# Seven stationary operands of a two-block transformer step placed at other byte remainders

## The reference

```python
def memory_cross_attention(h, mem_h, w_xq, w_xkv, w_xo):
    kv = mem_h @ w_xkv            # mem_h: 256 memory rows of 2048; w_xkv 2048 x 4096
    ...
def conv_glu_ffn(h, w_gate, w_up, conv_w, conv_b, w_down):   # first block, D_FF = 5632
    gate = causal_dwconv(h @ w_gate, conv_w, conv_b)
    return (jax.nn.silu(gate) * (h @ w_up)) @ w_down
def second_block(...):            # its feed-forward, D_FF_2 = 8192
    h = modulate(rms_norm_2(x, pre_norm_ffn[l]), shift_f, scale_f)
    f = jnp.square(jax.nn.relu(h @ w_up[l])) @ w_down[l]
```

## Time and profile before

| | |
|---|---|
| Median of three runs | 2789.39 us |
| Lowest and highest run | 2787.94 and 2789.61 us |
| Span of the profiled execution (first to last instruction) | 2785.1 us |
| TensorE matmuls busy | 2725.2 us, 98% of the span, 13302 matmuls |
| TensorE weight loads busy | 2329.5 us, 84% |
| VectorE, ScalarE busy | 1772.1 us, 1324.0 us |
| Mean granted TensorE clock | 0.993 |

### The profile page before, as it was taken

One profiled execution on the slowest core, in us unless ns is written; L12 is line 12 of the kernel. 1 busy time (PEld: TensorE's weight loads), 2 busy tenths in 40 slices (PEclk: granted clock), 3 DMA queues, 4 the chain that ended last, 5 costly groups with the idle time before them and its releaser, 6 DMA issues.

```text
span 2785.1 us, 34787 instructions
## 1 busy us (share of the span) xinstructions
PE 2725.2 (98%) x13302; PEld 2329.5 (84%) x13302; DVE 1772.1 (64%) x2025; ACT 1324.0 (48%) x1679; POOL 169.5 (6%) x132
## 2 busy tenths in 40 slices
PE   8999999999999999999999999998989999999998
PEld 8999988888888888888888799887868888888887
DVE  4477488776578888765555564547775756645455
ACT  5555444454445454434455454446455344344443
POOL 0001620000000000000000002720000000000000
PEclk9999999999999999999999999999999999999999
DMA  8554068887477777775555556640755866755553
GB/s 284 164 170 131 1 242 275 290 278 261 164 259 273 273 279 272 274 257 182 194 182 200 181 188 204 200 151 1 259 180 197 280 204 238 261 189 177 191 185 132
DMA packets 293266, 579.60 MB, mean 208 GB/s; under 512 B 9168, under 2 KB 46192, under 8 KB 292112
## 3 DMA queue, kind: packets, MB, share of 16 engines
q1 hardware_dynamic: 291296, 566.08, 60.4%
q0 software_dynamic: 1120, 8.57, 0.8%
q10 hardware_dynamic: 720, 3.15, 0.3%
HBM read 575.66 MB, written 2.10 MB: 207 GB/s over the span
## 4 chain that ended last, share of the span: by engine, by line
PE 95%; DVE 3%; ACT 1%; issue 1%; DMA 0%; SPq 0%; POOL 0%; DVEq 0%; ACTq 0%
PE GP L1006 28%; PE GP L1008 28%; PE GP L1007 28%; PE TA L959 2%; PE TB L959 2%; PE TB L607 1%; PE TB L426 1%; PE GP L401 0%; PE TA L1375 0%; DVE wlo L1960 0%; PE GP L1216 0%; PE TA L1216 0%; PE GP L1203 0%; DMA x<-in_x 0%; DVE x L2402 0%
## 5 line engine op out<-in xcount | busy, mean ns | idle before, releaser
L1960 DVE TENSOR_TENSOR wlo<-raw,whi 128x1024 fp32r<-128x1024 f32 (+2 forms) x904 | 1088.2, 1217 | 812.2 <-ACT whi L1468 803.2
L1468 ACT CAST whi<-raw 128x1024 fp32r<-128x1024 f32 (+2 forms) x904 | 923.7, 1029 | 1170.8 <-PE GP L1008 1109.5
L1006 PE MATMUL GP<-whi,hhi 128*128 128x512 f32 (+2 forms) x1792 | 689.9, 385 | 1.9 <-issue 1.4
L1008 PE MATMUL GP<-whi,hlo 128*128 128x512 f32 (+2 forms) x1792 | 681.6, 380 | 0.0
L1007 PE MATMUL GP<-wlo,hhi 128*128 128x512 f32 (+2 forms) x1792 | 680.8, 380 | 0.0
L1006 PEld LDWEIGHTS GP<-whi,hhi 128*128 128x128 f32 x1792 | 338.1, 189 | 52.2 <-issue 3.3
L1008 PEld LDWEIGHTS GP<-whi,hlo 128*128 128x128 f32 x1792 | 337.8, 188 | 52.0
L1007 PEld LDWEIGHTS GP<-wlo,hhi 128*128 128x128 f32 x1792 | 338.3, 189 | 50.5 <-issue 1.0
L1006 PE MATMUL GP<-whi,bhi 128*128 128x512 f32 x704 | 277.0, 393 | 0.2 <-DVE blo L2021 0.2
L1948 DVE SCALAR_TENSOR_TENSOR ada_acc<-raw,csig,ada_acc 128x512 f32<-128x512 f32 x360 | 270.3, 751 | 10.2
L1008 PE MATMUL GP<-whi,blo 128*128 128x512 f32 x704 | 274.6, 390 | 0.0
(11 more groups left out here) (437 smaller groups left out, 2578.2 us busy)
## 6 DMA issues: line engine op xcount, KB each, us to landing
raw<-in_w_up SPq DMA_DIRECT2D x108, 1024.0 KB, 5.4
raw<-in_w_down SPq DMA_DIRECT2D x108, 1024.0 KB, 5.1
raw<-in_w_ada SPq DMA_DIRECT2D x96, 1024.0 KB, 5.2
raw<-in_w_gate SPq DMA_DIRECT2D x44, 1024.0 KB, 5.3
raw<-in_w_in SPq DMA_DIRECT2D x48, 856.0 KB, 4.7
raw<-in_w_xkv SPq DMA_DIRECT2D x32, 1024.0 KB, 5.7
raw<-in_w_in SPq DMA_DIRECT2D x24, 1024.0 KB, 5.0
raw<-in_w_in SPq DMA_DIRECT2D x24, 864.0 KB, 4.7
```

What stands on the lines that cost most here:

```text
L1006: pe.matmul(o, ahi[:, kt, t], whi[r][:, k, 0:q.width], start=first, stop=False)
L1008: m = pe.matmul(o, alo[:, kt, t], whi[r][:, k, 0:q.width], start=False, stop=last)
L1468: nc.scalar.copy(whi[(2 * g + s) % NRING][:, :, 0:q.width], raw[j % NSLOT][:, 2 * s:2 * s + 2, 0:q.width])\
L1960: TTo(wlo[r][:, :, 0:q.width], raw[j % NSLOT][:, 2 * s:2 * s + 2, 0:q.width], whi[r][:, :, 0:q.width].bitcast(F32), ALU.subtract).then_inc ...
```

## The change

Only addresses change; no instruction is added or taken away. `level` gets a second argument, the bytes past the remainder of `ring0`. The new remainders are: `mhi` 128, `mlo` 256, `bhi` 32, `blo` 64, `flo` 192, `f2hi` 16 (4 elements) and `f2lo` 8 (2 elements). `hhi`, `hlo` and `fhi` (which lies over `hhi`) stay.

```diff
-        def level(at):
-            return at + (ring0 - at) % 4096
+        def level(at, past=0):
+            return at + (ring0 + past - at) % 4096
@@
-        ar = Arena(); ar.at = level(arena0 + 4 * NH * 2 * D)
-        mhi = ar("mhi", [P, KT, T], F32R); mlo = ar("mlo", [P, KT, T], F32R)
+        ar = Arena(); ar.at = level(arena0 + 4 * NH * 2 * D, 128)
+        mhi = ar("mhi", [P, KT, T], F32R)
+        ar.at = level(ar.at, 256)
+        mlo = ar("mlo", [P, KT, T], F32R)
@@
-        ar = Arena(); ar.at = level(arena0)
-        bhi = ar("bhi", [P, KT, T], F32R); blo = ar("blo", [P, KT, T], F32R)
+        ar = Arena(); ar.at = level(arena0, 32)
+        bhi = ar("bhi", [P, KT, T], F32R)
+        ar.at = level(ar.at, 64)
+        blo = ar("blo", [P, KT, T], F32R)
+        ar.at = level(ar.at, 192)
         fhi = nc.alloc_sbuf_tensor_at("fhi", [P, 24, T], F32R, offset=hh0); flo = ar("flo", [P, 24, T], F32R)
@@
-        f2hi = ar("f2hi", [P, 16, T], F32R); f2lo = ar("f2lo", [P, 16, T], F32R)
+
+        def shifted(name, n):
+            return ar(name, [P, 16 * T + n], F32R)[:, n:].rearrange("p (a b) -> p a b", b=T)
+
+        f2hi = shifted("f2hi", 4)
+        f2lo = shifted("f2lo", 2)
```

## The result

The changed kernel takes 2804.93 us (median of 4, 2802.82 to 2809.17) against 2788.66 us for the kernel before in the same comparison: a ratio of 1.0061, 95% interval 1.0049 to 1.0074, so 0.6% slower, a small loss but a clear one. The forecast of no change did not hold, though the time lies inside the stated range of 2773 to 2807 us, near its upper end; the rival with late loads had named 2805.6 us. The span went from 2785.1 to 2803.2 us, +18.1 us. (A launch has 1.8 us around its span, not the 4.3 us given above: 2805.0 against 2803.2 us here, and a run of the kernel before with the span 2785.1 us took 2786.86 us.)

The account below looks back on a forecast made before the run. TensorE was taken to bound the kernel, its 512-wide matmuls 0.2266 us apart. All terms were 0: 2785.1 us of span plus 4.3 us around it gave 2789.4 us, with a range of 2773 to 2807 us.

Parts of the forecast that it names:

- The forecast of no change: Whole kernel: the chip sees nothing of the moved addresses, time stays 2789.4 us; chance 0.56.
- the rival with late loads: Loads of moved arrays outlast their room, distance 230.0 ns, 2805.6 us; chance 0.22 together with a doubled `f2lo` load.
- What bounds the kernel: Whole span: TensorE, with 512-wide matmuls 0.2266 us apart at 2.4 GHz, never waiting for data in four runs.
- The nanosecond price of the prediction: 4768 of 13302 matmuls have a moved stationary operand; each nanosecond on their distance is 4.8 us.
- Stationary reads at the new places: Reads of moved hi and lo arrays by 4768 matmuls: claimed to cost or gain 0.
- The bounds of -63.4 and +16.2 us: Stationary reads on 4768 matmuls: gain at most 13.3 ns each, loss 3.4 ns each from the stretch behind transposes.
- The eight pairs of the earlier trace: Stationary and moving remainders over kt = 0..3 and both halves: one equal, seven 512 to 3584 bytes apart, all at 0.2266 us.
- Weight loads: Loads of 188 ns under 512-wide matmuls: about 30 ns of room, read from 196.3 ns at 428 columns; cost 0.
- The rule on 16-byte lines: Stationary rows: only `f2lo`, at 8 bytes, touches 33 lines instead of 32, a thirty-second of a covered load.
- The rule on the issue gap: 512-column matmuls: 518 cycles against 544 in the trace; if placement caused the 26, about 52 us gain on 4768.
- The small chance of 0.07 for such a gain: Rival that TensorE's reads get out of each other's way, 2726 us in full; chance 0.22, 0.07 for more than half.
- Writers, order, waits: ScalarE and VectorE write the same shapes, queue order stays; `f2lo` at +10% is 2 us, hidden; gain and loss 0.

## Why the prediction was right or wrong, point by point

*What bounds the kernel.* Right: the time moved with the distance of the matmuls and with nothing else. The nanosecond price of the prediction (4768 matmuls) counted only those whose own piece moved; in f the whole triple slowed, 1056 instead of 352, while f2's 1536 stayed. One array off level shows on all three matmuls of a triple.

*Stationary reads at the new places, taken as 0.* This is the step that failed. It measured +18.0 us, from between 4.3 and 6.0 ns on 3936 matmuls; over the 4768 the mean distance moved by 3.1 ns, past the 1.2 ns that the prediction named as its own sign of being wrong. The bounds of -63.4 and +16.2 us missed it by 2 us on the upper side. That the time is inside the stated range all the same is luck: its upper end came from late loads, which were not at work, and f2's 1536 matmuls, counted in it, cost nothing. Both reasons for the 0 were true and did not bear. The eight pairs of the earlier trace rows differ by multiples of 512, so all have remainder 0 of 256: they show one case eight times. The fp32 matmuls of line 1203 do differ by 32, and are not disturbed (0.89 us for eight in both halves), but they are another kind of matmul, 128 columns wide. The prediction named the gap itself ("what no float32r row shows is a difference that is not a multiple of 512") and still gave the rows that lay across the gap more weight than the open bound.

*Weight loads, taken as 0 because of 30 ns of room.* Right: the records stay at 188 ns, and the room behind them grew from 36 to 43 ns in m. The rival that had the sign and nearly the size right, the loads getting late, had the wrong mechanism, and its 230.0 ns from behind the transposes came near 231 to 233 by chance. What the traces show in its place is that the distance grows when the addresses of the stationary and the moving read are not a multiple of 256 bytes apart, and mostly by 233.3 - 226.7 = 6.6 ns, 16 cycles of 2.4 GHz per matmul; the most was 7.5 ns, in f at 96/96. That the two reads meet in the memory is what is left when the place itself, the absolute address, the loads' length and the writers are ruled out; no row shows the meeting itself. The 196.3 ns at 428 columns, by which the prediction measured the room, is one of two values there: of the ten long stretches of the kernel before (46 distances and more) five are at 193.3 ns, also with loads of 188 ns.

*The rule on 16-byte lines* (the Trainium skill, "SBUF — State Buffer", "Door 1: The DMA port swizzle"): 32, 64 and 192 are whole lines and cost, so it does not explain the loss. The table in the same page's section "A bandwidth-pool intuition that's wrong (but worth ruling out)" gives LDWEIGHTS a second independent read port. Two ports there may be; the distances of 231 to 233 ns show that the two reads are not free of each other in this stream.

*The rule on the issue gap* (the Trainium skill, "TensorE: Matmul & The Clock Gate", "Back-to-back issue gap"): it gave 518 cycles, 26 fewer than measured. No placement tried here brought a run of 512-wide matmuls under 226.7 ns, so nothing here shows that those cycles come from the placement. The small chance of 0.07 for such a gain was right.

*Writers, order, waits.* Right: `bhi` and `blo` take 471 and 478 ns in the median at their new places, within 3 ns of before, `f2lo` 1227 against 1226 ns, and no new wait of VectorE or DMA appeared.

*The rivals' shares.* No change had 0.56 and slower 0.22. Given that the one question that mattered had no row, slower deserved more: level placement was the only one whose float32r distance had been seen.

## What to carry to other kernels

Keep the stationary array and the moving tile of a dense float32r stream a multiple of 256 bytes apart in each partition; with arrays that start at multiples of 32 bytes it costs at most 224 bytes of padding for each, and here 4096-byte levelling buys nothing beyond it. Before calling a placement harmless, ask whether the rows in hand vary it at the grain of the change: a hundred pieces at multiples of 512 are one sample. And read TensorE by the distance of starts, since the shown durations have modelled ends (by line they moved by 2 to 7 ns of some 390 in the three products) and the load records do not move.

## What the runs showed that was not expected

- The distance takes few values. In long stretches at 512 columns it is 226.7 to 226.9, 228.9, about 231.1, 231.8 to 232.6, 233.3 or 234.3 ns; 233.3 is much the commonest away from 0. 8 bytes off (0/8, 231.1) costs as much as 64 off (0/64).
- 16/40 can run free, at 231 or at 233.3 ns, from one stretch to the next, and 16/0 and 16/16 do the same. 0/16 and 40/40 ran free only in short stretches of 22 or 23 distances. No free stretch was seen for 0/8, for 40/16 or for any pair off by multiples of 32. That the changed kernel's f2 was always in the free one (1536 matmuls at 226.7) saved it some 10 us, an estimate at 6.6 ns each; in other kernels the same pair was at 227.5 to 228.6. What decides the distance at the start of a stretch stays open, as does the law by which hi and lo combine (192/192 at 228.9 is less than 0/192 at 231.1).
- At 428 columns the distance is 193.3 or about 196.0 ns, stretch by stretch: before, five long stretches at each. With `hhi` and `hlo` at 32 all ten are at 193.3 to 193.5. But the longest of them (382 distances) also ran at 193.3 in the run with only the lo arrays of m, b, f and f2 moved, where `hhi` and `hlo` were level. So it is not shown that the shift did it; on 1152 matmuls it would be worth 2.4 us, under what can be measured here.
- The first matmuls behind an interruption are slower in both layouts, less so off level: in b the first 24 distances of a stretch are at 227.7 ns and the later ones at 226.7 before, at 231.7 and 231.1 after. The 230.0 ns of the earlier trace rows, over 12 distances, is the dearer end of that.
